# Attention on one core: a third buffer of probabilities, and the exponential of a round ahead of the high part of an older round on ScalarE

## The reference

```python
def gqa_attend(q, k, v):        # 8 heads of 128 in 2 groups; 512 queries, 768 keys
    s = jnp.einsum('bqkgd,bskd->bkgqs', q, k).astype(jnp.float32) * (q.shape[-1] ** -0.5)
    p = jax.nn.softmax(s, axis=-1).astype(v.dtype)
    return jnp.einsum('bkgqs,bskd->bqkgd', p, v)

o = lax.map(lambda qblk: gqa_attend(qblk, k_all, v_all), qb)
y_lat = o.swapaxes(0, 1).reshape(bsz, n_lat, GA_N_HEADS * hd) @ w_out
```

## Time and profile before

| | |
|---|---|
| median of 3 runs | 1569.68 us (1565.46 to 1570.1) |
| profiled execution, its own time | 1570.97 us |
| its span | 1569.2 us |
| mean granted TensorE clock | 0.942 of full speed |
| TensorE busy | 1377.1 us (88%) |
| VectorE busy | 959.4 us (61%) |
| ScalarE busy | 615.3 us (39%) |
| GpSimd busy | 171.4 us (11%) |
| first and last exponential of the attention stage start at | 248.6 and 355.1 us |

### The profile page before, as it was taken

How to read it: one execution, slowest core, us unless ns; L and a number is a source line. 1 busy time by engine, 2 the same in 40 slices (tenths; PEclk the granted TensorE clock), 3 DMA queues, 4 the chain that set the end, 5 groups by cost and what they waited for, 6 DMA issues and landing times. The chain is left out here.

```text
span 1569.2 us, 17367 instructions
## 1 busy us (share of the span) xinstructions
PE 1377.1 (88%) x6214; PEld 1091.4 (70%) x6214; DVE 959.4 (61%) x1262; ACT 615.3 (39%) x929; POOL 171.4 (11%) x150
## 2 busy tenths in 40 slices
PE   7997997888679999999958787888876999999995
PEld 1455786777458888888836676777754888888884
DVE  5786786886965555555567778877537333333344
ACT  2234545663344342534324334233324435243430
POOL 0503220002510000000330000000142000000022
PEclk9998999999879999999978988989997999999998
DMA  8443332105626565565211122121220322223221
GB/s 332 146 173 121 109 113 89 32 23 183 206 70 203 185 198 193 186 205 179 94 54 66 56 93 81 67 68 41 90 71 27 108 94 94 94 94 107 94 80 54
DMA packets 47373, 179.34 MB, mean 114 GB/s; under 512 B 6007, under 2 KB 6263, under 8 KB 43800
## 3 DMA queue, kind: packets, MB, share of 16 engines
q1 hardware_dynamic: 44312, 165.55, 31.3%
q0 software_dynamic: 3008, 13.11, 2.6%
HBM read 165.53 MB, written 10.49 MB: 112 GB/s over the span
## 5 line engine op out<-in xcount | busy, mean ns | idle before, releaser
L1432 PE MATMUL bank<-hhi,whi 128*128 128x512 f32 x864 | 343.6, 398 | 34.8 <-DVE hlo L985 22.4
L1434 PE MATMUL bank<-hhi,wlo 128*128 128x512 f32 x864 | 339.9, 393 | 0.0
L1433 PE MATMUL bank<-hlo,whi 128*128 128x512 f32 x864 | 339.8, 393 | 0.0
L972 DVE TENSOR_TENSOR wlo<-raw,whi 128x1024 fp32r<-128x1024 f32 x180 | 234.8, 1307 | 67.9 <-ACT whi L647 65.4
L1432 PE MATMUL bank<-ghi,whi 128*128 128x512 f32 x576 | 224.9, 390 | 4.6 <-DVE glo L1371 4.6
L1433 PE MATMUL bank<-glo,whi 128*128 128x512 f32 x576 | 224.5, 390 | 0.0
L1434 PE MATMUL bank<-ghi,wlo 128*128 128x512 f32 x576 | 224.5, 390 | 0.0
L1432 PEld LDWEIGHTS bank<-hhi,whi 128*128 128x128 f32 x864 | 164.2, 190 | 81.3 <-issue 30.6
L647 ACT ACTIVATE whi<-raw 128x1024 fp32r<-128x1024 f32 x180 | 188.6, 1050 | 6.4 <-DMA raw<-in_wpack 5.6
L1434 PEld LDWEIGHTS bank<-hhi,wlo 128*128 128x128 f32 x864 | 164.3, 190 | 34.8
L1433 PEld LDWEIGHTS bank<-hlo,whi 128*128 128x128 f32 x864 | 164.6, 190 | 32.6
(11 more groups left out here) (250 smaller groups left out, 2072.6 us busy)
## 6 DMA issues: line engine op xcount, KB each, us to landing
raw<-in_wpack SPq DMA_DIRECT2D x180, 512.0 KB, 3.4
araw<-in_apack SPq DMA_DIRECT2D x40, 512.0 KB, 3.4
amore<-in_apack SPq DMA_DIRECT2D x36, 512.0 KB, 3.3
ablk<-in_ahead SPq DMA_DIRECT2D x8, 1024.0 KB, 8.6
spectra<-scratch SPq DMA_DIRECT2D x8, 1024.0 KB, 4.2
araw<-spectra POOLq DMA_DIRECT2D x8, 1024.0 KB, 5.1
fs<-in_decay SPq DMA_DIRECT2D x8, 256.0 KB, 3.7
scratch<-in_decay SPq DMA_DIRECT2D x8, 256.0 KB, 3.0
```

The costliest lines, as they stand in the source:

```text
L972: TT(wlo[:, s, :], raw[:, r, :], f(whi[:, s, :]), ALU.subtract).then_inc(lo_done, 1)
L1432: mm(o, lh, rh, start=first, stop=False)
L1433: mm(o, lh, rl, start=False, stop=False)
L1434: return mm(o, ll, rh, start=False, stop=last)
```

## The change

It gives PROB a third buffer (rows 4 and 5 of the scratch tile), makes rsum and rinv three wide, and moves the four statements B and X on ScalarE ahead of H: in an iteration n, B(n-1) and X(n-1) come before H(n-3). X(m) now waits for T(m-3) in place of T(m-2). VectorE's and TensorE's lists keep their order; only the number of the buffer changes in them, and N(m)'s wait for an older N is one further back.

```diff
--- before.py
+++ after.py
@@ -116,8 +116,8 @@
         gain = sb("gain", [P, 2, 4, KC])
         gainc = sb("gainc", [P, KC])
         nmax = sb("nmax", [P, 2])
-        rsum = sb("rsum", [P, 2])
-        rinv = sb("rinv", [P, 2])
+        rsum = sb("rsum", [P, 3])
+        rinv = sb("rinv", [P, 3])
         asum = sb("asum", [P, ADA_QUARTER])
         qg = sb("qg", [P, 1])
         rq = sb("rq", [P, NH * QT])
@@ -352,7 +352,7 @@
 
         XH = [S[:, 4 + j % 4, :] for j in range(KC)]
         YC = [y[:, j, :] for j in range(KC)]
-        PROB = [S[:, 2 * n:2 * n + 2, :].rearrange("p a b -> p (a b)")[:, 0:NK] for n in range(2)]
+        PROB = [S[:, 2 * n:2 * n + 2, :].rearrange("p a b -> p (a b)")[:, 0:NK] for n in range(3)]
 
         FP, FP_, FQ, FQ_ = (araw[:, n // 2, n % 2 * NT:(n % 2 + 1) * NT] for n in range(4))
         UNIT_RAW = (es[:, 0, :], tap2[:, 0, :])
@@ -777,6 +777,16 @@
                     act.wait_ge(pv_done, m + 1)
                     A(hhi[:, m // 2, (m % 2) * 2 * P:(m % 2 + 1) * 2 * P], (B2, B3)[m % 2][:, 0:2 * P],
                       ACT.Copy).then_inc(ohi_done, 1)
+                m = n - 1
+                if 0 <= m < NQ:
+                    act.wait_ge(nmax_done, m + 1)
+                    if m >= 3:
+                        act.wait_ge(pt_done, m - 2)
+                    if m == 0:
+                        act.wait_ge(rq_done, 1)
+                    own(A(bmax[:, m % 2:m % 2 + 1], nmax[:, m % 2:m % 2 + 1], ACT.Copy, scale=rq[:, m:m + 1]))
+                    A(PROB[m % 3], score(m), ACT.Exp, bias=bmax[:, m % 2:m % 2 + 1], scale=rq[:, m:m + 1],
+                      accum_out=rsum[:, m % 3:m % 3 + 1]).then_inc(exp_done, 1)
                 m = n - 3
                 if 0 <= m < NQ:
                     act.wait_ge(pt_done, m + 1)
@@ -784,16 +794,6 @@
                         act.wait_ge(pv_done, m // 2 - 1)
                     A(phi[:, m // 2 % 2, :, (m % 2) * P:(m % 2 + 1) * P],
                       turned(m).rearrange("p (b c) -> p b c", b=KT), ACT.Copy).then_inc(phi_done, 1)
-                m = n - 1
-                if 0 <= m < NQ:
-                    act.wait_ge(nmax_done, m + 1)
-                    if m >= 2:
-                        act.wait_ge(pt_done, m - 1)
-                    if m == 0:
-                        act.wait_ge(rq_done, 1)
-                    own(A(bmax[:, m % 2:m % 2 + 1], nmax[:, m % 2:m % 2 + 1], ACT.Copy, scale=rq[:, m:m + 1]))
-                    A(PROB[m % 2], score(m), ACT.Exp, bias=bmax[:, m % 2:m % 2 + 1], scale=rq[:, m:m + 1],
-                      accum_out=rsum[:, m % 2:m % 2 + 1]).then_inc(exp_done, 1)
                 if n == 1:
                     act.wait_ge(csum_done, 1)
                     A(crow[:, 0:NT], B2[:, :], ACT.Copy).then_inc(crow_done, 1)
@@ -1191,10 +1191,10 @@
                 m = n - 2
                 if 0 <= m < NQ:
                     dve.wait_ge(exp_done, m + 1)
-                    if m >= 2:
-                        dve.wait_ge(p_done, m - 1)
-                    own(nc.vector.reciprocal(rinv[:, m % 2:m % 2 + 1], rsum[:, m % 2:m % 2 + 1]))
-                    TS(PROB[m % 2], PROB[m % 2], rinv[:, m % 2:m % 2 + 1], None, ALU.mult).then_inc(p_done, 1)
+                    if m >= 3:
+                        dve.wait_ge(p_done, m - 2)
+                    own(nc.vector.reciprocal(rinv[:, m % 3:m % 3 + 1], rsum[:, m % 3:m % 3 + 1]))
+                    TS(PROB[m % 3], PROB[m % 3], rinv[:, m % 3:m % 3 + 1], None, ALU.mult).then_inc(p_done, 1)
                 m = n - 3
                 if 0 <= m < NQ:
                     dve.wait_ge(phi_done, m + 1)
@@ -1587,7 +1587,7 @@
                     pe.wait_ge(exp_done, min(n - 1, NQ))
                     for kt in range(KT):
                         ins = nc.tensor.transpose(turned(m)[:, kt * P:(kt + 1) * P],
-                                                  PROB[m % 2][:, kt * P:(kt + 1) * P], ident)
+                                                  PROB[m % 3][:, kt * P:(kt + 1) * P], ident)
                     ins.then_inc(pt_done, 1)
                 if n < NQ:
                     h, qt = divmod(n, QT)
```

## The result

The changed kernel takes 1583.61 us (median of 4 runs, 1582.65 to 1588.2) against 1568.33 us for the kernel before beside it (1565.46 to 1570.1): a ratio of 1.0105, interval 1.0079 to 1.0131. It is slower by 15.3 us between the medians, 16.5 us by the ratio; the forecast was 1586, with a range from 1581 to 1594.

A forecast was written before the change was run, and what follows sets the result against it. Waits between engines were taken to bound the kernel, at 3.50 us a round. To the profiled 1570.97 us it added 14.6 for the stage and 1.8 for the clock, 1587.4, or 1586 against the median; range 1581 to 1594.

The forecast's parts named there:

- What bounded the kernel before: Attention stage: no engine is full; waits between engines set the pace, 3.50 us a round, with two different rounds alternating.
- the alternation of 3.88 and 3.11: Attention stage: TensorE works 3.88 us without a stop in rounds with PV; rounds without PV take a 3.11 us chain.
- the chain of 3.11: Rounds without PV: transposes, H, B, X, then the next transposes, 3.11 us.
- The ring: New order, attention stage: X, H, L, M, B and X again close in one round, 4.02 us against 3.50; +14.6 us.
- The third buffer at no cost: Third buffer, wider rsum and rinv: no added instruction, no late wait, cost nothing; allows X to go first.
- The start: Start of the attention stage: X(2) no longer waits for the first transposes, so X(3) comes earlier; -0.9 us.
- The tail: End of the stage: last but one PV waits for L(29), 2.8 us after X(31) in place of 1.9; +0.9 us.
- The clock: TensorE gaps of 2.7 us once in two rounds may lower its clock; 3 falls of 0.6 us taken, +1.8.
- The sum: Whole kernel: +14.6 us for the stage with its ends and +1.8 for the clock, giving 1586.
- VectorE bound: Faster rival, chance 0.03: the ring is not closed and VectorE sets 3.05 us a round; -13 us, 1557.
- the pace was not the old one: Rival that the move does nothing, chance 0.04: X still waits for its maximum, pace stays 3.50; 1569.7 us.
- the prediction's price for all 14: Rival, chance 0.12: the clock falls at most TensorE gaps; +8.4 us at all 14, +23 in total, 1593.

The follow-up runs named there:

- the halves: Kernel before, old order and two buffers, with each PV cut into two groups of 9 matmuls and O behind X: 1556.95 us against 1569.58, ratio 0.9923.
- the order alone: Kernel before with only B and X moved ahead of H, still two buffers: 1586.28 us against 1569.58, ratio 1.0111.
- the changed kernel with PV in halves: Changed kernel with each PV cut in two over odd and even iterations, and O behind H: 1582.12 us against 1567.52, ratio 1.008.
- the extra instruction beside the ring: Changed kernel with one more VectorE instruction per iteration from 4 to 31, behind M(n): 1586.6 us against 1567.52 for the kernel before, ratio 1.0111.
- the instruction inside the ring: Changed kernel with the same extra VectorE instruction ahead of M(n), behind L(n-3): 1588.64 us, ratio 1.013 to the kernel before.
- the ring opened: Changed kernel with M(n) ahead of L(n-3) in VectorE's list: 1571.23 us against 1569.58 for the kernel before, ratio 1.0014.
- six matmuls more behind PV: Changed kernel with six extra matmuls ahead of the transposes in even iterations: 1585.3 us against 1567.52 for the kernel before, ratio 1.0095.
- the buffer alone: Changed kernel with three buffers but ScalarE's list in the old order: 1569.97 us against 1569.58 for the kernel before, ratio 0.9998.

## Why the prediction was right

- **What bounded the kernel before.** Right, and shown by the halves: with PV spread out the alternation of 3.88 and 3.11 goes, and every round takes the chain of 3.11 (3.14 measured, with O moved as well).
- **The ring.** Forecast 4.02 a round, measured 4.00: X to H 0.99 as taken, H to L 0.83 against 0.85, L to M 0.87 against 0.88, M to B 0.99 against 0.98. The hand-over from M to B, which no row of the middle had shown, took 0.04. That it is this ring is shown by three runs: the order alone brings it, taking M out from behind L removes it, and 0.2 us put between L and M lengthens it by 0.2, while behind M it does not.
- **The third buffer at no cost.** Right. What it was said to allow was wrong in the plain rounds past the start; at a fall of the clock it spares some 0.43 us.
- **The ends.** The start was to give 0.9 and the profiled execution gave 0.3 (8.23 us from X(0) to X(3) against 8.55). M(3) had to wait for its scores to 254.76, since the clock was at 0.50 from 252 to 254 us, where before it was at 1.00. The start itself was worked out rightly: the changed kernel with PV in halves has the same program up to there, had the clock at 1.00, and took 7.57 us from X(0) to X(3), 0.98 less than before. What failed is the unspoken premise that the clock would stay up. The tail was to cost 0.9 and cost 0.5 (12.72 us from X(31) to the last O against 12.25); PV did start 2.83 us after X(31), as worked out, against 1.90. The rest of the tail hangs on where the clock falls: it took 10.24 to 13.12 us in the other runs with the new order and whole PVs, so a difference of 0.4 says nothing.
- **The clock.** Three falls of 0.6 us were taken, 1.8. The profiled execution had five long rounds of some 0.45 more, 2.3. The place of the price, O behind a slow PV with B behind O, was right, and so nearly was its size (O 1.53 us late less a slack of 1.07, for 1.6 less 1.0). The count was a guess and came out low: five falls at eight gaps of 2.7 us. It varies from run to run: with the order alone there was one, at twelve such gaps.
- **The sum.** From X(0) to the last O it is +16.5 us in the profiled executions (-0.3, +14.0 for 28 turns, +2.3, +0.5), forecast +16.4. The medians differ by 15.3. That the sum agrees to 0.1 us is luck in part: the ring was taken 0.6 too long and the tail 0.4 too dear, the start 0.6 too cheap and the clock 0.5. The spans differ by 17.2; the other 0.7 us lies ahead of X(0) (-0.7) and behind the last O (+1.5), where nothing was changed.
- **The rivals.** No VectorE bound came, and the pace was not the old one. The rule of the Trainium skill, "TensorE: Matmul & The Clock Gate", section "A second HAM failure mode: psum-queue depth-cycling", is borne out in part: the clock did go back and forth, in five rounds of 28, at five of 14 pairs of rounds, for 2.3 us where the prediction's price for all 14 was 8.4. The kernel before, with gaps of 1.84 us, never showed it in these rounds.

## What to carry to other kernels

Before an instruction is moved ahead of another on one engine, follow the one that falls behind through all the lists until you come back: if the path returns to the moved instruction in the same iteration, its links add up to a round, and a buffer that none of its links waits for, as the third one here, does not shorten it. Do the same with the cure: M ahead of L opened this ring and closed others. Here the wait that the trace showed (transposes for the exponential) was real, but it was paid in every second round only, and the cure was to spread the work of the other round, which makes the kernel 12 us faster. The busy shares said nothing of either; the spacing of one instruction through a stage tells the pace to 0.01 us, where the total hardly tells 2 us.

## What was not expected of the hardware

Behind equal gaps between groups of matmuls, with only transposes in them, the granted clock fell at some and not at others. In the profiled executions, between 260 and 366 us: gaps of 2.7 us were followed by a fall five times in eight in the changed kernel, five in nine with the extra instruction beside the ring, and once in twelve with the order alone; gaps of 2.9 us, with the instruction inside the ring, six times in seven. The gaps of 1.6 us (halves in the new order), 1.8 (the kernel before), 1.9 (the ring opened) and 2.1 (six matmuls more behind PV) had none behind them. At the start of the stage the clock was at 0.50 from 252 to 254 us after the change and at 1.00 before it, although TensorE had waited 2.92 us ahead of the first transposes in both. This fall is not the new order's: the old order with halves had it too (X(2) 3.80 us behind X(1) against 3.14), and the new order with halves did not. What decides it stays open. The tail of the kernel before, where the prediction had found its fall, is as little fixed: with the buffer alone and the same order the clock stayed at 1.00 there.
